# Routing of a mixture-of-experts decoder: exponentials moved ahead, clears and evictions given to other engines, one more final state in the wait for the sorted list

## What is computed

```python
def retention_step(r, qi, ki, vi):                    # 4 heads, dk 256, dv 512
    scores = einsum("bhtd,bhsd->bhts", qi, ki) * decay_mask
    out = einsum("bhts,bhse->bhte", scores, vi) + einsum("bhtd,bhde->bhte", qi, r) * xi
    r_new = r * chunk_decay + einsum("bhsd,bhse->bhde", ki * zeta, vi)   # the last one is an output
    return r_new, out

def hier_moe(x):                                      # 4 groups of 8 experts
    g_w, g_idx = top_k(softmax(x @ w_router_group + b), 1)
    e_val, e_idx = top_k((x @ w_router_expert + b)[g_idx], 2)
    e_w = softmax(e_val) * g_w
    for each of the 32 experts, its tokens:
        y += e_w * (silu(x @ w_gate) * (x @ w_up)) @ w_down
```

## Time and profile before

| | us |
|---|---|
| median of three runs | 1609.2 (1608.85 to 1611.48) |
| span of the profiled execution | 1605.9 |
| PE busy | 1565.6 (97% of the span), granted clock 0.995 of 2.4 GHz on average |
| DVE, ACT, POOL busy | 869.9, 275.5, 57.2 |
| share of PE in the chain that ended last | 86% |
| DMA traffic | 461.41 MB, 287 GB/s on average |

### The profile page before, as it was taken

How to read it: one execution, slowest core, us unless ns; L and a number is a source line. 1 busy time by engine, 2 the same in 40 slices (tenths; PEclk the granted TensorE clock), 3 DMA queues, 4 the chain that set the end, 5 groups by cost and what they waited for, 6 DMA issues and landing times.

```text
span 1605.9 us, 24827 instructions
## 1 busy us (share of the span) xinstructions
PE 1565.6 (97%) x9958; PEld 1080.8 (67%) x9958; DVE 869.9 (54%) x1812; ACT 275.5 (17%) x566; POOL 57.2 (4%) x103
## 2 busy tenths in 40 slices
PE   6999999999999999999999999999999998999997
PEld 3899888765698544444459999886649965444443
DVE  2676764565753454334457768556475434434436
ACT  3210000112200431111131100011121033111111
POOL 0000000001001100000000000000010001000000
PEclk9999999999999999999999999999999999999999
DMA  9734575488943799999983446535896438999993
GB/s 397 299 133 158 218 281 235 158 346 336 416 147 132 284 393 421 421 421 421 423 344 139 155 156 265 207 114 238 329 395 252 158 119 332 422 421 421 422 421 143
DMA packets 49810, 461.41 MB, mean 287 GB/s; under 512 B 5968, under 2 KB 6224, under 8 KB 10144
## 3 DMA queue, kind: packets, MB, share of 16 engines
q1 hardware_dynamic: 44656, 414.38, 64.5%
q10 hardware_dynamic: 3456, 37.75, 5.6%
q0 software_dynamic: 1584, 7.69, 1.2%
HBM read 415.88 MB, written 43.91 MB: 286 GB/s over the span
## 4 chain that ended last, share of the span: by engine, by line
PE 86%; issue 7%; DMA 3%; DVE 2%; ACT 1%; POOL 1%; DVEq 0%; SPq 0%; POOLq 0%; ACTq 0%
PE ps L795 86%; DMA state_sample_out<-ring 1%; DMA ring<-stream 1%; ACT work L1255 1%; DMA ovd<-sorted_rows 0%; DVE rope L1577 0%; DMA sorted_rows<-work,packed_rows 0%; DVEq L1521 0%; DMA cst<-consts 0%; POOL sorted_rows L761 0%; POOL kzm L741 0%; POOL rstd L709 0%; DVE hT L2129 0%; DVE hT L1595 0%; ACT L1255 0%
## 5 line engine op out<-in xcount | busy, mean ns | idle before, releaser
L795 PE MATMUL ps<-ring,work 128*64 128x512 f32 x1536 | 339.3, 595 | 2.8 <-ACT work L1255 2.8
L795 PEld LDWEIGHTS ps<-ring,work 128*64 128x64 f32 x1536 | 113.3, 137 | 211.2 <-issue 209.4
L795 PE MATMUL ps<-work,ring 128*128 128x160 f32 (+2 forms) x1600 | 231.4, 307 | 0.0
L1255 ACT ACTIVATE work<-ps 128x256 f32<-128x256 f32 (+5 forms) x238 | 102.3, 444 | 741.8 <-PE ps L795 733.2
L795 PEld LDWEIGHTS ps<-work,ring 128*128 128x128 f32 x1600 | 217.4, 191 | 13.4
L795 PE MATMUL ps<-ring,hT 128*32 128x128 f32 (+2 forms) x1776 | 171.4, 313 | 5.0 <-ACT hT L1255 5.0
L795 PE MATMUL ps<-hT,ring 128*128 128x160 f32 (+2 forms) x1024 | 169.7, 320 | 0.8 <-DMA ring<-stream 0.8
L795 PEld LDWEIGHTS ps<-hT,ring 128*128 128x128 f32 x1024 | 149.3, 191 | 17.7 <-issue 2.9
L795 PEld LDWEIGHTS ps<-ring,hT 128*32 128x32 f32 (+1 forms) x1776 | 126.8, 132 | 42.9 <-issue 29.3
L795 PE MATMUL ps<-work 128*128 128x288 f32 (+3 forms) x608 | 152.1, 393 | 3.4 <-DVE hT L2103 2.6
L795 PEld LDWEIGHTS ps<-work 128*128 128x128 f32 (+1 forms) x608 | 100.7, 185 | 53.9 <-issue 26.9
(11 more groups left out here) (222 smaller groups left out, 1169.6 us busy)
## 6 DMA issues: line engine op xcount, KB each, us to landing
ring<-stream SPq DMA_DIRECT2D x194, 1024.0 KB, 10.8
ring<-stream SPq DMA_DIRECT2D x95, 2048.0 KB, 8.9
state_sample_out<-ring ACTq DMA_DIRECT2D x16, 2048.0 KB, 9.1
state_out<-prm ACTq DMA_DIRECT2D x8, 512.0 KB
work<-sorted_rows SPq DMA_DIRECT2D x6, 512.0 KB, 5.1
prm<-params SPq DMA_DIRECT2D x1, 2608.5 KB, 27.7
prm<-params POOLq DMA_DIRECT2D x1, 2608.5 KB, 16.6
cst<-consts SPq DMA_DIRECT2D x1, 1651.0 KB, 21.0
```

Of the source, the lines that this page charges most:

```text
L795: return nc.tensor.matmul(out, lhsT, rhs, start=start, stop=stop, **k)
L1255: return act.activation(out, in_, func, **k)
```

## The change

All four final states are late: `f` 0 leaves retention. In routing, ACT's exponentials move from the step `gather` to the step `place`; `offsets` comes before the late final states; the list's tiles are evicted by ACT (left halves) and DVE (right halves); the fold of the last modulation stands ahead of `gather`; the diagonals are a step of their own, `diag`, after it. `hT` and the end of `hg` are cleared by POOL. `busy` falls from 9 to 6 in layer 0 and from 19 to 11 in layer 1.

```diff
-LATE_FINAL = [(1, 2, 3), (1, 2, 3)]
+LATE_FINAL = [(0, 1, 2, 3), (0, 1, 2, 3)]
...
-        + [("r1", 0), ("gb", 0), ("st", 4), ("y", 0), ("f", 0), ("fout", 0), ("kt", 1), ("sc", 1), ("st", 5), ("r1", 1), ("y", 1)]
+        + [("r1", 0), ("gb", 0), ("st", 4), ("y", 0), ("kt", 1), ("sc", 1), ("st", 5), ("r1", 1), ("y", 1)]
...
-        + ([("f", 1), ("fout", 1), ("place", 0), ahead[2], ahead[3], ("ob", 0), ("f", 3), ("fout", 3), ("busy", 9)] if l == 0
-           else [("f", 3), ("fout", 3), ("place", 0), ("f", 1), ("fout", 1), ("ob", 0), ("busy", 19)])
-        + [("gather", 0), ("offsets", 0), group]
+        + ([("f", 1), ("fout", 1), ("place", 0), ahead[2], ("ob", 0), ahead[3], ("offsets", 0), ("f", 3), ("fout", 3), ("f", 0), ("fout", 0), ("busy", 6)] if l == 0
+           else [("f", 3), ("fout", 3), ("place", 0), ("f", 1), ("fout", 1), ("ob", 0), ("offsets", 0), ("f", 0), ("fout", 0), ("busy", 11)])
+        + [group, ("gather", 0), ("diag", 0)]
...
+        kz_first = cut(prm[:, ln_at + 2 * D:ln_at + 2 * D + 2 * DK], 2, DK)
+
+        def keys_of(i):
+            return kz_first if i == 0 else kz if i == 1 else kz_late[:, i - 2, :, :]
...
+                        pool.memset(hT[:, :, :], 0.0).then_inc(cleared, 1)
+                    elif kind == "gather":
+                        for h in LATE_FINAL[l]:
+                            wait_made(pool, (l, ("f", h), "f1"))
+                        pool.memset(hg[:, :, PACK:HGW], 0.0).then_inc(cleared, 1)
...
-                    elif kind == "gather":
+                    elif kind == "place":
                         for n in range(2):
                             act.wait_ge(exp_in, l * 2 + n + 1)
...
+                    elif kind == "gather":
                         act.wait_ge(offsets_ready, l + 1)
...
-                            for half in range(2):
-                                out = wait_made(act, (l, step, f"s{t}{half}"))
-                                taken(apply(hg[:, 4 * half:4 * half + 4, t * P:t * P + rows], cut(out[:, :], 4, P)[:, :, 0:rows], ACT.Copy), (l, step, f"s{t}{half}"))
+                            out = wait_made(act, (l, step, f"s{t}0"))
+                            taken(apply(hg[:, 0:4, t * P:t * P + rows], cut(out[:, :], 4, P)[:, :, 0:rows], ACT.Copy), (l, step, f"s{t}0"))
...
+                act.wait_ge(cleared, 2 * l + 2)
...
-                wait_made(dve, (l, ("htok", 0), "h5"))
-                dve.memset(hT[:, :, :], 0.0)
-                dve.memset(hg[:, :, PACK:HGW], 0.0)
...
+                    elif kind == "gather":
+                        for t in range(SORTED):
+                            rows = min(P, PACK - t * P)
+                            out = wait_made(dve, (l, step, f"s{t}1"))
+                            taken(dve.tensor_copy(hg[:, 4:8, t * P:t * P + rows], cut(out[:, :], 4, P)[:, :, 0:rows]), (l, step, f"s{t}1"))
+                    elif kind == "diag":
+                        diagonals(l)
                 assert n_var == VARS
+                dve.wait_ge(cleared, 2 * l + 1)
```

More of the change, by code:

```diff
@@ L73, in layer_steps @@
         + [("gr", 0), ("st", 0), ("gr", 1), ("st", 1), ("gr", 2), ("st", 2), ("gr", 3), ("st", 3)]
[1 row of a table removed]
-        + [("kt", 2), ("sc", 2), ("st", 6), ("r1", 2), ("y", 2), ("kt", 3), ("sc", 3), ("st", 7), ("r1", 3), ("y", 3)] + ([] if 3 in LATE_FINAL[l] else [("f", 3), ("fout", 3)])
[2 rows of a table added]
         + [("ysum", 0), ("gb", 1), ("bts", 0)] + [("bt", i) for i in range(8)]
@@ L146, in tiles_of @@
         return [f"s{t}{half}" for t in range(SORTED) for half in range(2)]
-    if kind in ("va", "ysum", "offsets", "ssq", "scale", "affine", "fold", "rstd", "busy", "fout"):
+    if kind in ("va", "ysum", "offsets", "ssq", "scale", "affine", "fold", "rstd", "busy", "fout", "diag"):
         return []
@@ L477, in build @@
         hg = X(KT, HGW)
-        ot1, ot2 = W(place[0], NOVER, NE), W(place[0] + NOVER * NE, NOVER, NE)
+        ot1, ot2 = W(place[0] + 2 * TOK + 12 * NE, NOVER, NE), W(place[0] + 2 * TOK + 12 * NE + NOVER * NE, NOVER, NE)
         pick12, above = W(place[0] + 2 * TOK, 2, 3, NE), W(place[0] + 2 * TOK + NOVER * NE, 3, NE)
@@ L544, in build @@
         packed_ready = sem("packed_ready")
+        cleared = sem("cleared")
         sorted_stored = sem("sorted_stored")
@@ L1055, in _ @@
                     elif kind == "f":
-                        keys = (kz if i < 2 else kz_late[:, i - 2, :, :])
+                        keys = keys_of(i)
                         for dt in range(2):
@@ L1814, in offsets @@
                     settle()
[L1816 to L1820, removed]
                 def over_blocks(ap):
@@ L1850, in offsets, with diagonals @@
                 dve.nop().then_inc(tables_ready, 1)
+            def diagonals(l):
+                dve.wait_ge(rf_stored, (l + 1) * 16 * HEADS)
+                for tt, rows in TTILES:
+                    eye = C("ident")[0:rows, 0:rows].rearrange("p (o t) -> p o t", o=1).broadcast_to([rows, 4, rows])
+                    last = dve.tensor_tensor(diag[0:rows, 4 * tt:4 * tt + 4, 0:rows], eye, spread(vals[0:rows, tt, :], rows), ALU.mult)
+                last.then_inc(counts_ready, 1)
             for s in (over_gu_made, over_hidden, over_down_made, over_sum_taken):
```

## The result

The changed kernel is slower: median 1614.85 us of 11 runs, against 1609.02 for the kernel before on the same chip. The ratio is 1.0037, 95% interval 1.0028 to 1.0046, so +4.5 to +7.4 us. One of the 11 took 3274 us at a granted clock of 1.00, against 0.991 to 0.996 in the others; it isn't in the ratio, and the median of the other ten is 1614.60. The profiled execution has a span of 1613.4 us, 7.5 more than before.

The account below looks back on a forecast made before the run. Full DMA engines were taken to bound the pair stage and `gb` 1's load in retention, though PE looked 97% busy. Terms -1.24 - 1.89 + 1.3 + 0.6 + 0.6 = -0.6 us gave 1608.6 us, range 1603.8 to 1611.2.

Parts of the forecast that it names:

- -1.24: Layer 0's retention: `gb` 1's load lands 1.24 us sooner, as a 512 KB store leaves at 421 GB/s.
- -1.89: Layer 1's retention: `gb` 1 starts 1.89 us sooner, 1.24 for the store plus 0.65 between landing and start.
- my bound of 0: Retention, each layer: worst case for `gb` 1's load, no gain because other stores, 3.5 us sooner, take the room.
- +1.3: Layer 0's `gb` 1: PE's clock falls after a longer stop, costing 1.3 us, bounds 0 and +1.7; layer 1 none.
- rival C: `gb` 1: TensorE's clock falls in both layers, adding 1.5 us: sum +0.9, time 1610.1; chance 0.10.
- a stop between 1.42 and 2.13 us: PE's clock: threshold from earlier routing stops; pair 0 kept pace after 1.42 us, the clock fell after 2.13.
- "+0.6" and "+0.6": Routing: the moved state's store costs 0.6 us on layer 0's full stream and 0.6 in layer 1's scatter.
- Exponentials, offsets, evictions, clears: 0 each: Routing: these parts gain 0 us each; an earlier pair 0 doesn't end the pairs earlier, as DMA sets their end.
- the pitch of 14.9 us: Pair stage: the DMA-set interval of 14.91 us between groups would begin some pairs earlier, a sign of being right.
- the bound: Clears on POOL: even at four times DVE's 1.98 us they would end before pair 1, costing 0.
- PE waits about 3 us in layer 0 and 1 to 2 in layer 1, both start 1 to 2 us sooner: Sign of being right, at `gb` 1: these waits come before it, and it starts sooner by that much.
- half the clock in layer 1: Sign of being wrong: PE's clock is halved in layer 1's `gb` 1, which would point to rival C.

Follow-up runs that it names:

- e3: Changed kernel with four unread products at the place head 0's final state left in retention, its store staying in routing: 1609.81 us, ratio 1.0011.
- e5: Changed kernel with the stores of sample states 6 and 7 held until `gb` 1's first products are made: 1604.26 us, ratio 0.9976.
- e2: Kernel before, with the store of head 0's final state cut from 512 KB to 8 KB in both layers: 1608.16 us, ratio 1.0000.
- e1: Changed kernel with head 0's final state back in retention and `busy` 9 and 19; the other changes stay: 1609.23 us, ratio 1.0002.
- e9: Kernel before, with the stores of sample states 6 and 7 held until `gb` 1's first products are made: 1608.39 us, ratio 0.9998.
- e8: Changed kernel with the store of head 0's final state cut from 512 KB to 8 KB: 1612.18 us, ratio 1.0032.
- e4: Changed kernel with four unread products directly in front of `gb` 1's own: 1610.18 us, ratio 1.0017.
- e10: Changed kernel with the stores of sample states 5, 6 and 7 held until `gb` 1's first products: 1624.51 us, ratio 1.0094.
- e11: Changed kernel with the stores of states 6 and 7 held and all list evictions back on ACT: 1603.85 us, ratio 0.9980.

## Why the prediction was wrong

The sum had 1608.6 and the range ended at 1611.2; the time is 1614.85. The sum was -0.6 us against the profile's +7.5 (+7.4 of it in the table): 4.9 us of the difference are the load, 3.1 the clock.

- **"-1.24" and "-1.89", the load lands sooner: the step that failed.** Measured +0.76 and +0.97 at `gb` 1's start, 4.9 us off together. I wrote that the sample states' stores, issued sooner, "move shares, not the total", and counted nothing. The total was right: from 404 to 416 the engines moved 419 GB/s before and 426 in the changed kernel. But PE waits for one transfer, not for the total, and its share is what moved: the stores of states 5 and 6 went out 3.3 us sooner, and `gb` 1's load took 13.4 instead of 12.3 us, in layer 1 13.0 instead of 11.5. e3 (old pace) and e5 (stores held) both remove it. Even my bound of 0 was no bound: it supposed that the stores could take at most the room that the 512 KB had left. e2 shows the second half of the error: taking out 512 KB didn't bring 1.24 us to the transfer that is waited for. Another store landed 2.2 us sooner, and the engines moved less at a full share.
- **"+1.3" for the clock: mechanism right, size wrong.** It came to +1.69 in layer 0 and +2.76 in layer 1, where I had 0. That is rival C's mechanism, which I gave 0.10, from a stop 2.5 times as long as it supposed (4.25 for 1.7 us). The two prices are half the time that the group runs on the lower level: about 3.4 us in layer 0 and 5.4 in layer 1, by the windows of 1 us above. My reading that the clock falls from a stop between 1.42 and 2.13 us on fits every case of `gb` 1: it held at 1.91 and fell at 2.17. It isn't general: pair 0 ran slow after stops of 1.19 (e1) and 1.22 us (e9), with other stops some us ahead, so the row of 1.42 us that it rested on the earlier trace rows was in part luck. And the length of the stop depended on the failed term.
- **Routing, "+0.6" and "+0.6".** Measured -0.70 + 1.06 = +0.4 in layer 0 and -0.06 + 0.96 = +0.9 in layer 1, together 1.3 for 1.2. The sum is right, in part by luck. Layer 1's term was a list 0.6 us later; from the last scatter issue to SP's first list load it takes 6.06 us, where it took 5.74, and 5.7 to 6.2 over all kernels with the state there. The loss came in the pair stage, where PE waits for a load (1.01 us in layer 0, 0.86 in layer 1), and e8 could not show that the store is behind it.
- **Exponentials, offsets, evictions, clears: 0 each.** Right as a sum, by e1. That an earlier pair 0 is given back in the pair stage was right too; where it is given back was not: the pitch of 14.9 us does not begin pairs earlier. In both kernels it starts with the same pair, and PE instead meets a load late near the end of the stage (1.01 us). Where pair 0 does start clearly sooner the sign appears: in e5, 3.65 us sooner counted from `gb` 0, it begins one pair earlier in layer 0 (692.80). The clears on POOL took 2.04 and 0.95 us, far from the bound.
- **"PE waits about 3 us in layer 0 and 1 to 2 in layer 1, both start 1 to 2 us sooner"**: 4.96 and 4.25, both later. Of the signs I had listed for being wrong, only half the clock in layer 1 appeared.

## What to carry to other kernels

When the DMA engines are full, taking work off an engine that also paces the issue of stores can make the next awaited load later: find the one transfer that is waited for, and list what else will be in flight beside it at the new pace, not only how many bytes leave. Then the order of transfers is the lever: holding two stores whose slots were not needed soon turned a loss of 6 us into a gain of 4, while holding one more, whose slot was needed, ended 16 us above the kernel before. Dividing the bytes taken out by the rate of the full engines doesn't price it. And a stop of PE can cost more than its length: filling it, even with products nobody reads, can pay until it is removed.

## What the hardware showed unexpectedly

- The same 2 MB load of `gb` 1 took 7.6 us with no store beside it, 10.4 with state 5's store beside it and the next two held, 12.3 before and 13.4 in the changed kernel (layer 0). The last two have the same stores beside it, of states 5 and 6, but state 6's runs beside it for 6.1 us before and for 10.3 in the changed kernel. In the 7.6 us case the next load wasn't beside it either, so that figure isn't the stores' alone.
- With one store fewer, engines at the same share moved less: 419 GB/s before and 354 in e2 over 12 us (1.00 and 0.99), 419 and 365 in layer 1, 367 in e3 in layer 0. A share of 1.00 isn't a rate.
- PE's clock in `gb` 1, over all the profiled executions here: after eleven stops of 0.19 to 1.91 us the group took 8.03 us, after stops of 2.17, 2.50, 3.26, 4.00, 4.96 and again 4.96 us 9.63 to 9.72. So the price was the same 1.6 to 1.7 us from 2.17 to 4.96 us of stop; only after 4.25 us did the group take 10.68 us, 2.65 more, once. Why it was more that time is open.
- In layer 0's routing ACT and DVE wait 4.4 to 4.6 us for a modulation product (557.26 above) that PE's rows show finished 2 to 3 us earlier, in the changed kernel, e1, e3, e4, e10 and e11. In e5 to e8 the same waits are 2.62 and 1.85 us and end with PE. What the longer ones wait for is not settled. They delay the start of `offsets`, and through DVE's evictions perhaps pair 0: compare e8 above.
